# Loads, splits and table sets moved in a fused two-block kernel on one Trainium2 core

## The reference

```python
# layer 0, input of the gated DeltaNet
proj = h @ w_in                                  # q, k, v, z: 8 heads of 128 each; a, bt: 8 columns each
qkv = silu(causal_dwconv(qkv, conv_w))           # 4 taps
beta = sigmoid(bt)
g = -exp(a_log) * softplus(a + dt_bias)
gc = cumsum(g, axis=-1)                          # per chunk of 64 positions
rhs = concatenate([v * beta, kb * exp(gc)])      # v is needed with positions on the rows
sol = triangular_solve(kk + eye, rhs)
# second block, experts: top 2 of the 8 in the best of 8 groups
y[token] += gate * (silu(x @ w_gate[e]) * (x @ w_up[e])) @ w_down[e]
# w_gate, w_up: 1024x512; w_down: 512x1024; 2 MB each in float32, 64 experts
```

## Time and profile before

| what | value |
| --- | --- |
| median of 3 runs | 3437.37 us (3436.29 to 3437.51) |
| profiled execution | 3432.18 us, its span 3430.5 us |
| mean granted TensorE clock | 0.938 |
| PE busy | 3024.0 us (88%) |
| DVE busy | 1118.0 us (33%) |
| ACT busy | 783.8 us (23%) |
| POOL busy | 871.9 us (25%) |
| moved by DMA | 630.79 MB, mean 184 GB/s |

### The profile page before, as it was taken

How to read it: one execution, slowest core, us unless ns; L and a number is a source line. 1 busy time by engine, 2 the same in 40 slices (tenths; PEclk the granted TensorE clock), 3 DMA queues, 4 the chain that set the end, 5 groups by cost and what they waited for, 6 DMA issues and landing times. The chain is left out here.

```text
span 3430.5 us, 39129 instructions
## 1 busy us (share of the span) xinstructions
PE 3024.0 (88%) x15618; PEld 1989.4 (58%) x15618; DVE 1118.0 (33%) x1848; ACT 783.8 (23%) x1110; POOL 871.9 (25%) x730
## 2 busy tenths in 40 slices
PE   5998789999899989999989779997888888888887
PEld 2777568877688757787769666445333333333333
DVE  2565565571530052422251455533101010101102
ACT  1334532231322242322333431111000000000001
POOL 0442135444354313444424122000111111111110
PEclk9999889999999999999989888998999999999999
DMA  6224335452223302233312121012999999999996
GB/s 231 86 76 133 100 111 174 169 178 80 68 93 98 92 13 86 74 98 101 85 55 86 38 73 53 0 71 91 377 407 415 417 410 408 411 409 405 407 402 276
DMA packets 254499, 630.79 MB, mean 184 GB/s; under 512 B 18821, under 2 KB 208294, under 8 KB 229105
## 3 DMA queue, kind: packets, MB, share of 16 engines
q1 hardware_dynamic: 243569, 618.68, 48.1%
q0 software_dynamic: 10240, 8.43, 0.8%
q10 hardware_dynamic: 576, 2.10, 0.2%
HBM read 633.33 MB, written 20.97 MB: 191 GB/s over the span
## 5 line engine op out<-in xcount | busy, mean ns | idle before, releaser
L418 POOL TENSOR_TENSOR ring_parts<-ring,arena_parts 128x512 fp32r<-128x512 f32 x544 | 709.3, 1337 | 1163.4 <-ACT arena_parts L394 1006.9
L526 PE MATMUL ps<-arena_parts,arena_parts 128*128 128x512 f32 (+1 forms) x2080 | 784.2, 377 | 86.6 <-POOL ring_parts L418 47.8
L528 PE MATMUL ps<-arena_parts,ring_parts 128*128 128x512 f32 (+1 forms) x2080 | 772.9, 372 | 0.0
L3743 PE MATMUL ps<-arena 128*64 128x512 f32 x1024 | 514.6, 661 | 160.7 <-DMA arena<-in_w_up 102.4
L527 PE MATMUL ps<-hT_parts,arena_parts 128*128 128x512 f32 (+1 forms) x1728 | 630.9, 365 | 0.0
L3744 PE MATMUL ps<-arena 128*64 128x512 f32 x1024 | 516.0, 663 | 0.0
L526 PEld LDWEIGHTS ps<-arena_parts,arena_parts 128*128 128x128 f32 x2080 | 397.5, 191 | 177.4 <-POOL ring_parts L418 51.8
L528 PEld LDWEIGHTS ps<-arena_parts,ring_parts 128*128 128x128 f32 x2080 | 397.8, 191 | 71.5
L3743 PEld LDWEIGHTS ps<-arena 128*64 128x64 f32 x1024 | 149.9, 152 | 494.2 <-issue 492.4
L527 PEld LDWEIGHTS ps<-hT_parts,arena_parts 128*128 128x128 f32 x1728 | 330.1, 191 | 51.2
L394 ACT ACTIVATE arena_parts<-ring 128x2048 fp32r<-128x2048 f32 (+1 forms) x105 | 210.7, 2007 | 413.3 <-PE ps L528 369.1
(11 more groups left out here) (555 smaller groups left out, 3436.1 us busy)
## 6 DMA issues: line engine op xcount, KB each, us to landing
arena<-in_w_down SPq DMA_DIRECT2D x64, 2048.0 KB, 23.5
arena<-in_w_gate SPq DMA_DIRECT2D x63, 2048.0 KB, 19.0
arena<-in_w_up SPq DMA_DIRECT2D x63, 2048.0 KB, 22.9
ring<-in_ffn_up SPq DMA_DIRECT2D x44, 1024.0 KB, 5.1
arena<-in_ada_w SPq DMA_DIRECT2D x12, 2048.0 KB, 10.0
ring<-in_ret_w_in SPq DMA_DIRECT2D x24, 1024.0 KB, 5.3
ring<-in_ffn_down SPq DMA_DIRECT2D x16, 1408.0 KB, 7.1
ring<-in_gdn_w_in SPq DMA_DIRECT2D x16, 1024.0 KB, 6.0
```

The costliest lines, as they stand in the source:

```text
L418: ins = pool.tensor_tensor(lower[:, at], whole[:, at], upper[:, at], ALU.subtract)
L526: pe.matmul(out, upper[:, r], self.upper[r][:, part], start=(r == 0), stop=False)
L528: ins = pe.matmul(out, lower[:, r], self.upper[r][:, part], start=False, stop=(r == self.tiles - 1))
L3743: pe.matmul(k.ps[upper, 2 + u, :], m.xeT[u][:, r, :], m.w_up[u][:, r, :], start=(r == 0), stop=(r == KD - 1))
```

## The change

Five things change.

1. In the experts' stage, gate and up weights get a third buffer each, which serves expert 2 alone: `w_gate[2]` lies in `hT` and `w_up[2]` in `hn`. SP issues the first after the router has turned the last tile, the second after the rows of x are out (`load_up_apart`). Expert 3 then uses buffer 0 and expert 4 buffer 1, so from expert 3 on an expert's projection buffers are 1 - u. SP's order is now gate and up of 0 and 1, down 0, down 1, gate and up of 2, gate and up of 3, down 2, gate and up of 4, down 3, gate and up of 5, and so on. The last expert's second halves share the semaphore `apart_in`.
2. In `DeltaIn`, the gate columns are split as other weights are (ACT rounds, DVE subtracts, after the input's split) and the logits are 24 split products in one bank, in PE's stream behind group 1. The rest of the gates moves behind group 1 on DVE (`decay_rows`) and behind chunk 0 on ACT (`gates`), where chunk 2 is rounded ahead of it. DVE no longer makes `x` before it splits the input.
3. Turning v has new places: even heads 0, 2, 4, 6 behind groups 27, 28, 29, 30 and odd heads 1, 3, 5, 7 amid groups 28, 29, 30, 31, between the fourth and the fifth K tile. ACT leaves heads 2j and 2j + 1 behind group 27 + j.
4. In `DeltaHeads`, `leave_join(0)` stands ahead of the two calls of `keys`.
5. Table loads: the one at the head of `ResidualNorm.scalar` stays only where the stage starts anew and its input is not yet there, which takes it out of three of the four stages; the lower bounds of the forget gates come at group HYT, one later; the one at the head of the HGRN heads is gone.

```diff
@@ -858,6 +858,8 @@
+        self.w_parts = [k.as_parts(self.tiles[:, 2 * GH + n, :].rearrange("p (r c) -> p r c", r=KD)) for n in range(2)]
+        self.gate_parts = Signals(k, "input", rounded=1, split=1)
@@ -874,6 +876,12 @@
+    def logits(self, half):
+        return self.k.ps[half * self.SUB:half * self.SUB + GH, 4, :]
@@ -900,14 +908,18 @@
-        pe.wait_ge(k.sem("h_ready"), KD)
-        k.wait_tables(pe, "gdn")
-        for half in range(2):
+        pe.sem_inc(k.sem("gdn_convolved"), self.BANKS)
+
+        def logits():
+            self.gate_parts.wait(pe, "split", 1)
+            upper, lower = self.w_parts
+            out, last = k.ps[0:self.SUB + GH, 4, :], KD - 1
             for r in range(KD):
-                ins = pe.matmul(k.ps[0:GH, 4 + half, :], self.w_gate[:, r, half * GH:(half + 1) * GH], k.hT[:, r, 0:T],
-                                start=(r == 0), stop=(r == KD - 1))
+                w, v = upper[:, r, 0:self.SUB + GH], lower[:, r, 0:self.SUB + GH]
+                pe.matmul(out, w, self.input.upper[r], start=(r == 0), stop=False)
+                pe.matmul(out, w, self.input.lower[r], start=False, stop=False)
+                ins = pe.matmul(out, v, self.input.upper[r], start=False, stop=(r == last))
@@ -948,7 +960,7 @@
-        beside = {7: [(turn_gates,)], 6: [(sums, 0, 0)], 10: [(sums, 0, 1)], 14: [(sums, 1, 0)], 18: [(sums, 1, 1)]}
+        beside = {1: [(logits,)], 7: [(turn_gates,)], 6: [(sums, 0, 0)], 10: [(sums, 0, 1)], 14: [(sums, 1, 0)], 18: [(sums, 1, 1)]}
@@ -964,8 +976,13 @@
-        for h, g in enumerate((27, 28, 29, 29, 30, 30, 31, 31)):
-            beside.setdefault(g, []).append((turn_v, h))
+        amid = {}
+        for h in range(GH):
+            g = self.CONVOLVED + 3 + (h + 1) // 2
+            if h % 2:
+                amid[g] = lambda h=h: turn_v(h)
+            else:
+                beside.setdefault(g, []).append((turn_v, h))
@@ -978,7 +995,7 @@
-                ins = self.input.products(pe, k.ps[:, g % self.BANKS, :], upper[:, :, at], lower[:, :, at], g == 0)
+                ins = self.input.products(pe, k.ps[:, g % self.BANKS, :], upper[:, :, at], lower[:, :, at], g == 0, between=amid.get(g))
@@ -994,20 +1011,27 @@
-        dve.wait_ge(k.sem("gate_logits"), 2)
-        dve.tensor_scalar(x, k.ps[0:GH, 4, :], self.head[0:GH, 1, :], None, ALU.add).then_inc(k.sem("gate_x"), 1)
+        for n in range(2):
+            dve.tensor_copy(self.w_parts[n], self.window[:, 0:1].unsqueeze(1).to_broadcast([P, KD, 2 * self.SUB])).then_inc(k.sem("gate_cells"), 1)
         self.input.vector(dve)
-        dve.wait_ge(k.sem("gate_exp"), 2)
-        dve.tensor_scalar(e, e, 1.0, None, ALU.add).then_inc(k.sem("gate_x"), 1)
-        dve.wait_ge(k.sem("gate_exp"), 4)
-
-        st.done(dve.scalar_tensor_tensor(g, x, 0.0, e, ALU.max, ALU.add))
-        st.wait()
-        st.done(dve.tensor_scalar(g, g, self.head[0:GH, 0, :], -1.0, ALU.mult, ALU.mult))
-        st.wait()
-        for t in range(GCN):
-            at = slice(t * P, (t + 1) * P)
-            dve.tensor_tensor_scan(self.g_rows[:, at], one[:, at], g[:, at], 0.0, ALU.mult, ALU.add).then_inc(k.sem("gate_rows"), 1)
+        self.gate_parts.wait(dve, "rounded", 1)
+        upper, lower = (self.by_half(part) for part in self.w_parts)
+        dve.tensor_tensor(lower, self.w_gate.rearrange("p r (h c) -> p r h c", h=2), upper, ALU.subtract).then_inc(self.gate_parts.sem("split"), 1)
+
+        def decay_rows():
+            dve.wait_ge(k.sem("gate_logits"), 1)
+            dve.tensor_scalar(x, self.logits(0), self.head[0:GH, 1, :], None, ALU.add).then_inc(k.sem("gate_cells"), 1)
@@ -1064,7 +1088,7 @@
-        beside = {9: [(gate_columns,), (differences,)], 13: [(split_root, 0)], 17: [(split_gates,)], 21: [(key_scale,), (split_root, 1), (strengths,)]}
+        beside = {1: [(decay_rows,)], 9: [(gate_columns,), (differences,)], 13: [(split_root, 0)], 17: [(split_gates,)], 21: [(key_scale,), (split_root, 1), (strengths,)]}
@@ -1112,18 +1136,22 @@
-        act.wait_ge(k.sem("gate_logits"), 2)
-        act.activation(self.b_rows, k.ps[0:GH, 5, :], ACT.Sigmoid).then_inc(k.sem("gate_rows"), 1)
-        act.preload_act_table_set(LOG_TABLES)
...
+        act.wait_ge(k.sem("gate_cells"), 2)
+        act.activation(self.by_half(self.w_parts[0]), self.w_gate.rearrange("p r (h c) -> p r h c", h=2), ACT.Copy).then_inc(self.gate_parts.sem("rounded"), 1)
+
+        def gates():
+            act.wait_ge(k.sem("gate_logits"), 1)
+            act.activation(self.b_rows, self.logits(1), ACT.Sigmoid).then_inc(k.sem("gate_rows"), 1)
+            act.preload_act_table_set(LOG_TABLES)
+            act.wait_ge(k.sem("gate_cells"), 3)
@@ -1161,14 +1189,14 @@
-        for h, g in enumerate((28, 29, 30, 30, 31, 31, 31, 31)):
-            beside.setdefault(g, []).append((leave_v, h))
+        for h in range(GH):
+            beside.setdefault(self.CONVOLVED + 3 + h // 2, []).append((leave_v, h))
...
-            if c + 1 < self.CHUNKS:
+            if c != 1 and c + 1 < self.CHUNKS:
@@ -1181,6 +1209,9 @@
+            if c == 0:
+                round_chunk(2)
+                gates()
@@ -1608,9 +1639,9 @@
+        leave_join(0)
...
             keys(h)
-        leave_join(0)
@@ -1915,7 +1946,8 @@
-        act.preload_act_table_set(LOG_TABLES)
+        if self.first and not self.input.ready:
+            act.preload_act_table_set(LOG_TABLES)
@@ -2696,7 +2728,7 @@
-                    if g == HYT - 1:
+                    if g == HYT:
@@ -3453,12 +3484,15 @@
+        by_rows = lambda ap: ap.rearrange("p k n -> p (k n)")[:, 0:KD * D_EXP].rearrange("p (k n) -> p k n", k=KD)
...
+        self.w_gate.append(by_rows(k.hT[:]))
+        self.w_up.append(by_rows(self.hn))
@@ -3668,7 +3703,9 @@
-        with eng.Fori(1, NE // 2 - 1) as i:
+        for u in range(2):
+            step(1, u, True, True)
+        with eng.Fori(2, NE // 2 - 1) as i:
@@ -3678,14 +3715,21 @@
+            self.wait(sp, freed, e + 1 if after is None else after + 3)
...
+        def load_up_apart(e):
+            of = lambda src: k.ins[src][e:e + 1].rearrange("o (p k) n -> p (o k) n", p=P)
+            sp.wait_ge(k.sem("hn_turned"), TT)
+            sp.dma_start(m.w_gate[self.THIRD], of("w_gate_2")).then_inc(k.sem("apart_in"), 16)
+            sp.wait_ge(k.sem("x_rows_out"), 16 * TT)
+            sp.dma_start(m.w_up[self.THIRD], of("w_up_2")).then_inc(k.sem("apart_in"), 16)
@@ -3696,22 +3740,26 @@
-        load_up(2, 0)
         load_down(1, 1)
-        load_up(3, 1)
-        with sp.Fori(2, NE // 2 - 1) as i:
+        load_up_apart(self.THIRD)
+        load_up(3, 0, 0)
+        load_down(2, 0)
+        load_up(4, 1, 1)
+        load_down(3, 1)
+        load_up(5, 0)
+        with sp.Fori(3, NE // 2 - 1) as i:
             for u in range(2):
                 load_down(i * 2 + u - 2, u)
-                load_up(i * 2 + u, u)
+                load_up(i * 2 + u, 1 - u)
         load_down(NE - 4, 0)
-        load_up(NE - 2, 0)
+        load_up(NE - 2, 1)
...
-        load_up_halves(NE - 1, 1)
+        load_up_halves(NE - 1, 0)
@@ -3734,14 +3782,14 @@
-        def project(u, ahead, in_halves):
+        def project(u, b, ahead, in_halves):
...
-                    pe.wait_ge(k.sem("last_half_in"), 32)
-                pe.matmul(k.ps[upper, 2 + u, :], m.xeT[u][:, r, :], m.w_up[u][:, r, :], start=(r == 0), stop=(r == KD - 1))
-                ins = pe.matmul(k.ps[lower, 2 + u, :], m.xeT[u][:, r, :], m.w_gate[u][:, r, :], start=(r == 0), stop=(r == KD - 1))
+                    pe.wait_ge(k.sem("apart_in"), 64)
+                pe.matmul(k.ps[upper, 2 + u, :], m.xeT[u][:, r, :], m.w_up[b][:, r, :], start=(r == 0), stop=(r == KD - 1))
+                ins = pe.matmul(k.ps[lower, 2 + u, :], m.xeT[u][:, r, :], m.w_gate[b][:, r, :], start=(r == 0), stop=(r == KD - 1))
@@ -3766,8 +3814,17 @@
+            if isinstance(e, int) and e == self.THIRD:
+                b = self.THIRD
+                pe.wait_ge(k.sem("apart_in"), 32)
+            elif isinstance(e, int) and e < self.THIRD:
+                b = u
+                self.wait(pe, f"gate_in{b}", 16)
+                self.wait(pe, f"up_in{b}", 16)
+            else:
+                b = 1 - u
+                self.wait(pe, f"gate_in{b}", i * 16 + 16 * u)
+                self.wait(pe, f"up_in{b}", i * 16 + 16 * u)
@@ -3776,7 +3833,7 @@
+            project(u, b, ahead, not next)
```

More of the change, by code:

```diff
@@ L996, in vector @@
         dve.memset(self.window[:, self.SUB - 1:self.SUB], 1.0)
[L997 to L998 removed]
+        for n in range(2):
+            dve.tensor_copy(self.w_parts[n], self.window[:, 0:1].unsqueeze(1).to_broadcast([P, KD, 2 * self.SUB])).then_inc(k.sem("gate_cells"), 1)
         self.input.vector(dve)
[L1000 to L1010 removed]
+        self.gate_parts.wait(dve, "rounded", 1)
[4 more added lines that the diff above has]
+            dve.tensor_scalar(x, self.logits(0), self.head[0:GH, 1, :], None, ALU.add).then_inc(k.sem("gate_cells"), 1)
```

(27 more changed lines are left out.)

20 lines of the change are left out of this document (9 added, 11 removed).

## The result

The changed kernel takes 3392.93 us (median of 4 runs, 3391.40 to 3396.87) against 3436.83 for the kernel before in the same runs: a ratio of 0.9875, 95% interval 0.9864 to 0.9887. That is 43.9 us less, where 33.2 were forecast, and 1.1 us under the lower end of the range. Its profiled execution took 3391.40 us (span 3389.6), 40.8 less than that of before.

What follows compares the result with a forecast made beforehand. The experts' weight stream was taken to bound the last thousand microseconds, with engines waiting on each other before. Terms 12.2 + 9.3 + 7.6 + 1.5 + 2.6 = 33.2 us gave 3404.2, said as 3404; range 3394 to 3418.

Steps and rivals of the forecast that it cites:

- Bound and pace of the stream: Experts' stage: a stream of weights bounds it, w_up leading with 19% of the span; an earlier load is worth 5.26 us.
- A: Third expert's weights issued early in the experts' stage: 12.2 us gained, between 8 and 15.8, with one gap of 3.6 us.
- rivals 2 and 3: Experts' stage: weight queue empties several times, A falls to 4, 3412, 12%; w_down holds back up loads, about 3616, 3%.
- B: Logits of the first stage as split products behind group 1: 9.3 us gained, bounds 5 and 11.7.
- rival 1: First stage: VectorE's splits and the gate chain hold up chunks 2 and 3, B falls to 2: 3411, chance 13%.
- C: Turning v one head at a time, before the heads: 7.6 us gained, bounds 4 and 8.5.
- E: Table loads removed at the start of two residual stages: 2.6 us gained, between -1.3 and +3.8.
- rival 4: A removed table load is put back where functions change; E is nil or a loss of 2.6: 3407 to 3410, 5%.
- D: First join's copy ahead of the keys at the heads' start: TensorE's wait goes, 1.5 us gained, bounds 0 and 4.
- rival 5: More than said: TensorE keeps 2.4 GHz through the heads' start and no gap opens in the stream: 3396, chance 5%.

Runs made afterwards that it cites:

- no_e: The changed kernel with the table loads put back and the lower bounds one group earlier, at HYT - 1: 3400.94 us.

## Why the prediction was wrong, by its own steps

- **Bound and pace of the stream: right.** w_up leads the chain in both kernels, and a load made earlier was worth what it takes.
- **A, 12.2: right.** The four profiles give 12.2 to 12.6 against the first of before (13.0 between the means), with one gap of 3.1 us for 3.6 and TensorE's 12.0 us step; rivals 2 and 3 did not come. The gather of x was not held up: it starts at 2365.44 us, 27.9 earlier than before, as the stage does.
- **B, 9.3: right**, 9.3 by the step and 9.2 when undone. The contention of the two subtracting engines was sized from the earlier trace rows at 1.69 and 1.63 us and measured 1.65 and 1.63. The Trainium skill (SBUF — State Buffer, "Who interferes with whom") has the two exclude each other; strict turns would be 0.61 + 1.24 = 1.85 us a pair, so the trace agrees with the rule in kind, and a pair is 0.2 us shorter than strict turns. Group 2 was out at 87.8 us for 88.5, and its convolution began at 90.98 for 91, hidden by the banks as said; rival 1 did not come.
- **C, 7.6: right**, 7.4 by the step (8.2 between the means) and 7.3 alone. TensorE no longer waits in turning v, and the heads' first exponential (275.37 us) is 17.3 us earlier, as said. Undone in the changed kernel it costs 10.1, beside a dip of the clock.
- **E, 2.6: right in size**, 1.3 and 1.1 us against no_e in the two places. (Of the step of 2.0 at 1300 us in the table, no_e has 0.9 without the change.) No load was put back; rival 4 did not come.
- **D, 1.5 with bounds 0 and 4: this is the term that was mis-sized.** It measured 7.0 us as a step, 7.0 alone and 7.9 when undone. The step that failed is that only the wait would go: the prediction let the granted clock behind the wait stay at 0.50 as before. It named the mechanism ("TensorE might keep its clock") but set its bound at 4 without a row and gave it, inside rival 5, a chance of 5%. Of rival 5 this half came, and the other, no gap in the stream, did not. The trace of before had the price: the clock stood at 0.50 for 12 us in which TensorE was busy. If all of that work took half as long at 2.4 GHz, it would give 6 us back, and with the wait 7.5; 7.0 to 7.9 were measured. The likely case should have been that the pair follows its neighbours: a wait in the middle of its start goes, and nothing else makes TensorE idle there.
- **The base.** The sum was taken off 3437.4, the median of three executions. Of 48 executions of before in all runs the median is 3435.8; of ten of the changed kernel it is 3393.0, a difference of 42.8 us. Against 3435.8 the same sum would have said 3402.6.
- **The range and rival 5.** The bounds of A and B, from which 3394 is said to follow, reach only down to 3404.2 - 3.6 - 2.4 = 3398.2. The upper bounds of C and D, 0.9 and 2.5 more, would bring it to 3394.8. Rival 5, D at 4 and no gap, adds up to 3404.2 - 2.5 - 3.6 = 3398.1, not 3396. With D at 7 its two halves would have given 3395.1.

Of the 11.3 us by which 3404.2 missed, the base makes 1.6. The means of the four profiles' shifts at 3425 us are 2.9 and -38.3, so 41.2 us between the kernels, 8.0 more than the sum. Of these 8.0 D makes 5.7, and no other stretch more than 0.8. The medians of all executions differ by 42.8 us, so the last 1.6 us are in no profile. No run tells what they belong to; that one kernel draws more episodes of the low clock than the other is possible and not shown.

## What to carry to other kernels

A wait of a microsecond in a passage where TensorE already works with gaps can have two prices, as it had here: the wait of 1.5 us, and up to half of the busy time that follows at the lower clock, 5.5 to 6.4 us. Read the granted clock behind each short wait that a change removes or adds; the stretch at 0.50 that follows bounds the second price. And before a forecast to 0.3%, ask how far the few executions at hand stand from the kernel's others: here the profiled one was 3.6 us under the median of 48 and the median of three 1.6 us above it, which is as much as some of the edits are worth.

## What was not expected of the hardware

- 1.35 us of idle time decided whether TensorE ran the next 10 us at 1.2 or 2.4 GHz, and ten products with no use put in its place, 2.50 us of work, kept 2.4 GHz.
- The same instructions ran at 0.50 or at 1.00 in the Hyena part in different executions, and 100 us of work took 106.6 to 106.8 us then. The executions of the kernel before went from 3425.3 to 3441.1 us; the draws of the clock, and waits such as the 6.02 us at 525 us, are what their traces show to differ.
